# A two-block transformer on one core: attention's sums ahead of its turns, the mixers' low halves ahead of statistics and modulation, and the convolution as the last source of the mixers' output

## What is computed

```python
def gqa_mix(h_lat, h_ctx, ...):                 # block 1, layer 1: 8 heads of 128, 2 of k and v
    q_l = apply_rope(rms_norm(split_heads(qkv[..., :Q_DIM], N_HEADS), q_norm_g), cos, sin)
    k_all = jnp.concatenate([k_c, k_l], axis=2)
    y_lat = merge_heads(block_attend(q_l, k_all, v_all)) @ w_o

for l in range(DEPTH):                          # block 2
    mod = c_act @ ada_w[l] + ada_b[l]           # nine rows of 1024: shifts, scales, gates
    x = x + 0.5 * gt1 * _swiglu(_modulate(_rmsnorm(x, ffn1_norm[l]), sh1, sc1), ...)
    proj = _modulate(_rmsnorm(x, mix_norm[l]), sh2, sc2) @ mix_w_in[l]
    o_a = attention(rope(rmsnorm(a_q)), rope(rmsnorm(a_k)), a_v)   # 512 features, 8 heads of 64
    o_b = silu(group_layernorm(depthwise_conv31(a * sigmoid(g))))  # 256 features
    o_c = rmsnorm(gla(c_q, c_k, c_v, log_decay)) * silu(c_r)       # 256 features
    mixed = jnp.concatenate([o_a, o_b, o_c], axis=-1) @ mix_w_out[l]
    x = x + gt2 * mixed
    x = x + 0.5 * gt3 * _swiglu(_modulate(_rmsnorm(x, ffn2_norm[l]), sh3, sc3), ...)
```

## Time and profile before

| | us |
|---|---|
| median of 3 runs | 3186.99 |
| the runs | 3184.89 to 3188.21 |
| the profiled execution | 3188.7 |
| its span, first to last instruction | 3187.0 |
| PE busy in it | 3090.6 |

### The profile page before, as it was taken

One profiled execution on the slowest core, in us unless ns is written; L12 is line 12 of the kernel. 1 busy time (PEld: TensorE's weight loads), 2 busy tenths in 40 slices (PEclk: granted clock), 3 DMA queues, 4 the chain that ended last, 5 costly groups with the idle time before them and its releaser, 6 DMA issues.

```text
span 3187.0 us, 46876 instructions
## 1 busy us (share of the span) xinstructions
PE 3090.6 (97%) x19420; PEld 2751.5 (86%) x19420; DVE 2041.7 (64%) x2146; ACT 957.7 (30%) x1006; POOL 669.5 (21%) x616
## 2 busy tenths in 40 slices
PE   8999999999999999999997999999989999998999
PEld 5888889888888888888886798899879999997899
DVE  5844368666387434774556766675887758668664
ACT  2211122212222122221224433333533333354333
POOL 1311100224022010220102021330632313136110
PEclk9999999999999999999998999999999999999999
DMA  7633235332255332553523496685547868654464
GB/s 258 211 133 93 92 119 187 105 102 75 91 158 176 101 96 89 160 183 119 172 96 119 128 272 221 194 266 195 185 149 219 258 200 271 232 191 167 137 182 158
DMA packets 501669, 522.81 MB, mean 164 GB/s; under 512 B 15732, under 2 KB 433830, under 8 KB 501478
## 3 DMA queue, kind: packets, MB, share of 16 engines
q1 hardware_dynamic: 498536, 513.76, 50.4%
q0 software_dynamic: 2944, 6.32, 1.0%
HBM read 518.97 MB, written 1.05 MB: 163 GB/s over the span
## 4 chain that ended last, share of the span: by engine, by line
PE 86%; DVE 7%; POOL 3%; ACT 2%; DMA 1%; issue 1%; SPq 0%; DVEq 0%; ACTq 0%; POOLq 0%
PE ps L2191 29%; PE ps L2365 15%; PE ps L2277 15%; PE ps L2389 8%; PE ps L2219 6%; PE ps L2256 2%; DVE wl L1228 2%; PE ps L2235 1%; POOL wst L809 1%; PE ps L2662 1%; PE ps L2128 1%; POOL lnp L815 1%; PE ps L2303 1%; PE ps L2099 1%; DMA mraw<-in_ada_w 1%
## 5 line engine op out<-in xcount | busy, mean ns | idle before, releaser
L1228 DVE TENSOR_TENSOR wl<-wraw,wh 128x2048 fp32r<-128x2048 f32 x339 | 829.0, 2446 | 566.9 <-ACT wh L838 561.7
L838 ACT ACTIVATE wh<-wraw 128x2048 fp32r<-128x2048 f32 x341 | 652.5, 1913 | 945.7 <-PE ps L2277 387.5
L2191 PE MATMUL ps<-xh,wh 128*128 128x512 f32 (+1 forms) x1504 | 564.9, 376 | 0.5 <-DVE xl L1280 0.3
L2191 PE MATMUL ps<-xl,wh 128*128 128x512 f32 (+1 forms) x1504 | 552.7, 367 | 0.0
L2191 PE MATMUL ps<-xh,wl 128*128 128x512 f32 (+1 forms) x1504 | 551.3, 367 | 0.0
L2365 PE MATMUL ps<-xh,wh 128*128 128x258 f32 x1408 | 403.7, 287 | 5.3 <-DVE xl L1426 4.2
L2365 PE MATMUL ps<-xh,wl 128*128 128x258 f32 x1408 | 399.7, 284 | 0.0
L2365 PE MATMUL ps<-xl,wh 128*128 128x258 f32 x1408 | 399.3, 284 | 0.0
L673 POOL CAST hh<-ht 128x256 f32 (+1 forms) x176 | 140.1, 796 | 1227.1 <-DVE ht L1608 891.0
L1201 DVE SCALAR_TENSOR_TENSOR acc<-mraw,svec,acc 128x1024 f32<-128x1024 f32 x259 | 342.3, 1341 | 12.7 <-DMA mraw<-in_ada_w 5.2
L2191 PEld LDWEIGHTS ps<-xl,wh 128*128 128x128 f32 x1504 | 283.2, 188 | 49.3
(11 more groups left out here) (430 smaller groups left out, 5564.6 us busy)
## 6 DMA issues: line engine op xcount, KB each, us to landing
wraw<-in_ffn_w_in SPq DMA_DIRECT2D x352, 512.0 KB, 5.2
wraw<-in_ffn_w_out SPq DMA_DIRECT2D x176, 512.0 KB, 4.2
mraw<-in_ada_w SPq DMA_DIRECT2D x72, 1024.0 KB, 7.0
mraw<-in_w_mod SPq DMA_DIRECT2D x64, 1024.0 KB, 6.8
wraw<-in_gmlp_w_in SPq DMA_DIRECT2D x48, 512.0 KB, 4.5
wraw<-in_mix_w_in SPq DMA_DIRECT2D x48, 512.0 KB, 4.7
wraw<-in_gmlp_w_out SPq DMA_DIRECT2D x24, 512.0 KB, 3.9
first_w<-in_w_mod SPq DMA_DIRECT2D x8, 1024.0 KB, 11.6
```

The lines of the kernel that those rows point to most:

```text
L838: act.activation(wh[:, slot], wraw[:, slot], ACT.Copy).then_inc(whi_done, 1)
L1228: dve.tensor_tensor(wl[:, slot], wraw[:, slot], wh[:, slot].bitcast(F32), ALU.subtract)\
L2191: m = pe.matmul(ps[:, bank, 0:width], a, b, start=k == p == 0, stop=k == KD - 1 and p == 2)
```

## The change

- **Attention.** `queries(u)` falls into `query_sums(u)` and `query_turn(u)`; the sums stand one turn ahead, turns 1 and 2 stand together, turn 3 inside the head loop at head 0. POOL's two low halves (L796) go; DVE makes them inside the head loop at heads 2 and 4. ACT squares and splits earlier and runs a one-element exponential ahead of the first real one. The transposes of `q_1` write another bank.
- **Entry of block 2.** `keep_going` runs 20 products ahead of the wait for `y_evac` and 36 behind it, where 16 stood; `columns` stands behind the transposes.
- **Both mixers.** DVE's `split_next` of units 7, 9, 10, 11 and 12 stands ahead of sums, modulation or taps; DVE's taps (`taps(1)`) stand behind the split of unit 11; POOL's powers stand behind 7 and 10 taps (9 and 13 before). ACT takes over the copy and the squares of `o`, and the copies of `pt_c` and `pt_b`, and loads its tables ahead by one-element operations. `MIX_OUT` makes conv the last source; its statistics stand behind attention's low half. `columns(nxt, 1)` stands behind the scores, `columns(nxt, 2, 3)` behind `out(3)`. Modulation 10 stands between conv's low half and the last split, 12 and 13 behind that split. The next sublayer's order of input blocks (`MIXED`) changes.

```diff
-MIX_OUT = (3, 2, 0, 1)
+MIX_OUT = (3, 0, 1, 2)
-NATURAL, MIXED = tuple(range(8)), (0, 1, 4, 5, 6, 7, 2, 3)
+NATURAL, MIXED = tuple(range(8)), (0, 1, 2, 3, 6, 7, 4, 5)
-MIX_POOL_TAPS, MIX_DVE_TAPS = (9, 13, 24), (24, 28, 31)
+MIX_POOL_TAPS, MIX_DVE_TAPS = (7, 10, 24), (24, 28, 31)
...
-                    for i in (6, 7):
-                        u = s["n_unit"] + i
-                        pool.wait_ge(whi_done, u + 1)
-                        pool.tensor_tensor(wl[:, u % 2], wraw[:, u % 2], wh[:, u % 2].bitcast(F32), ALU.subtract)\
-                            .then_inc(wlo_done, 1)
...
+                    query_sums(0)
                     unit(3)
-                    queries(0)
+                    query_turn(0)
+                    query_sums(1)
                     unit(4)
-                    queries(1)
+                    query_sums(2)
+                    query_turn(1)
+                    query_turn(2)
                     maximum(0)
-                    queries(2)
+                    query_sums(3)
                     normalise(0)
                     maximum(1)
-                    queries(3)
                     normalise(1)
                     for h in range(HEADS):
                         if h + 2 < HEADS:
                             maximum(h + 2)
+                        if h == 0:
+                            query_turn(3)
+                        elif h == 2:
+                            unit(5)
+                        elif h == 4:
+                            unit(6)
                         if h in ATT_MODS:
                             mod_unit(nxt, 2, ATT_MODS.index(h))
...
-                    stage("o_copy", dve.tensor_copy(o_c, ps[:, 6].rearrange("p (t c) -> p t c", t=TT)))
-                    steps.link(dve.tensor_tensor(hx[:], o_c, o_c, ALU.mult))
...
                     stage("oc", dve.tensor_tensor(o_c, o_c, gg[:], ALU.mult))
-                    normalise("c", p_c, 0)
                     maximum("a", 0, 4, 12)
-                    MP.wait(dve, "conv", turn)
-                    steps.link(dve.tensor_copy(ctok.rearrange("p a b -> p (a b)"), ps[:, 7]))
-                    grp = ctok.rearrange("p t (g c) -> p (t g) c", c=64)
+                    low("gla", 6, (6,))
+                    normalise("b", p_b, 8)
+                    normalise("a", p_a[:], 12)
+                    split_next(u0 + 12)
+                    turned_weights("a", 0, slice(0, 2))
+                    low("att", 0, (0, 1))
                     for g in range(8):
                         m = steps.mark(dve.bn_stats(hst[:, g], grp[:, g]))
...
-                    split_next(u0 + 12)
+                    split_next(u0 + 13)
                     low("conv", 4, (2,))
+                    modulation(10)
+                    split_next(u0 + 14)
                     modulation(12)
-                    unit(13)
-                    low("att", 0, (0, 1))
-                    unit(14)
-                    unit(15)
+                    modulation(13)
...
+                    keep_going(3, 20)
                     pe.wait_ge(y_evac, s["n_group"])
+                    keep_going(3, 36)
+                    transposes(s)
                     columns(s, 2)
-                    keep_going(3, 16)
-                    transposes(s)
...
-                        MV.wait(pe, ("lo_gla", "lo_conv", "lo_att", "lo_att")[i], turn)
+                        MV.wait(pe, ("lo_gla", "lo_att", "lo_att", "lo_conv")[i], turn)
...
-                        if i == 2:
-                            columns(nxt, 2, 3)
...
-                    for i in range(1, 4):
-                        out(i)
+                    out(1)
+                    out(2)
+                    MA.wait(pe, "conv", turn)
+                    MP.done("convt", outputs_turned(512, 2))
+                    out(3)
+                    columns(nxt, 2, 3)
```

More of the change, by code:

```diff
@@ L1026, in _ @@
                     unit(3, False)
+                    square(1)
                     split_next(u0 + 4)
-                    square(1)
-                    copy_heads(0)
                     unit(4, False)
                     square(2)
+                    copy_heads(0)
+                    split_next(u0 + 5)
+                    act.activation(nrm1[:, 31:32], ones[:, 0:1], ACT.Exp)
+                    unit(5, False)
+                    square(3)
                     copy_heads(1)
                     exps(0)
-                    unit(5)
-                    square(3)
                     copy_heads(2)
@@ L1150, in _ @@
                     unit(10)
+                    MP.wait(act, "o", turn)
+                    stage("o_copy", act.activation(om[:, :, 768:1024], ps[:, 6].rearrange("p (t c) -> p t c", t=TT), ACT.Copy))
+                    stage("o_sq", act.activation(hx[:], om[:, :, 768:1024], ACT.Square))
                     exps("c", 2, p_c, 0)
-                    unit(11)
+                    split_next(u0 + 11)
                     exps("b", 4, p_b, 8)
+                    act.activation(table_scrap[:, 0:1], ones[:, 0:1], ACT.Silu)
+                    unit(11, False)
+                    act.activation(table_scrap[:, 1:2], ones[:, 0:1], ACT.Exp)
                     MP.wait(act, "omt", turn)
@@ L1156, in _ @@
                     exps("a", 0, p_a[:], 12)
+                    act.activation(table_scrap[:, 2:3], ones[:, 0:1], ACT.Silu)
+                    MP.wait(act, "pt_c", turn)
+                    MA.done("pt_c", act.activation(pt0[:, :, :, 0:P], ps[:, 2:4].rearrange("p r (h q) -> p r h q", h=4), ACT.Copy))
                     unit(12)
+                    MP.wait(act, "pt_b", turn)
+                    act.activation(pt0[:, :, 2:4, P:2 * P], ps[:, 2].rearrange("p (r h q) -> p r h q", r=2, h=2), ACT.Copy)
+                    MA.done("pt_b", act.activation(pt1[:, :, 2:4], ps[:, 3].rearrange("p (r h q) -> p r h q", r=2, h=2), ACT.Copy))
+                    MP.wait(act, "pv", turn)
+                    high("att", 0, (0, 1))
+                    unit(13)
                     MV.wait(act, "o_conv", turn)
@@ L1161, in _ @@
                     high("conv", 4, (2,))
-                    unit(13)
-                    MP.wait(act, "pv", turn)
-                    high("att", 0, (0, 1))
                     unit(14)
@@ L1976, in _ @@
                     turn_heads(0)
+                    split_next(u0 + 6)
+                    sum_squares(1)
                     modulation(5)
-                    sum_squares(1)
-                    unit(6)
-                    taps(1)
                     turn_heads(1)
                     split_next(u0 + 7)
-                    split_next(u0 + 8)
-                    modulation(7)
                     MA.wait(dve, "decays", turn)
@@ L2006, in _ @@
                     stage("kt_t", op)
-                    unit(9)
+                    modulation(8)
+                    split_next(u0 + 9)
+                    mod_end(nxt, 1, 6, 488)
                     MP.wait(dve, "scores", turn)
@@ L2026, in _ @@
                     stage("states", op)
-                    unit(10)
+                    split_next(u0 + 10)
+                    taps(1)
+                    modulation(9)
                     maximum("c", 2, 8, 0)
-                    MP.wait(dve, "o", turn)
+                    MA.wait(dve, "o_sq", turn)
                     o_c = om[:, :, 768:1024]
-                    stage("o_copy", dve.tensor_copy(o_c, ps[:, 6].rearrange("p (t c) -> p t c", t=TT)))
-                    steps.link(dve.tensor_tensor(hx[:], o_c, o_c, ALU.mult))
                     groups = nrm_g.rearrange("p (t h) -> p t h", t=TT)
@@ L2059, in _ @@
                     stage("stats", dve.tensor_tensor(grp, grp, hmv[:, :, 0:1].broadcast_to([P, 8, 64]), ALU.subtract))
-                    low("gla", 6, (6,))
-                    MP.wait(dve, "pt_c", turn)
-                    MV.done("pt_c", dve.tensor_copy(pt0[:, :, :, 0:P], ps[:, 2:4].rearrange("p r (h q) -> p r h q", h=4)))
-                    normalise("b", p_b, 8)
                     dve.wait_ge(rstd_ready, n_power[0])
@@ L2801, in _ @@
                     MP.done("pt_a", turn_weights(p_a[:], 0))
-                    MV.wait(pe, "pt_b", turn)
-                    MA.wait(pe, "conv", turn)
-                    MP.done("convt", outputs_turned(512, 2))
+                    MA.wait(pe, "pt_b", turn)
                     MV.wait(pe, "pt_a", turn)
```

79 lines of the change are left out of this document (42 added, 37 removed).

## The result

| | before | changed |
|---|---|---|
| median, us | 3185.94 (4 runs) | 3164.93 (4 runs) |
| the runs | 3183.42 to 3188.21 | 3163.78 to 3168.58 |
| span of the profiled execution | 3187.0 | 3166.8 |

The ratio is 0.9936 with a 95% interval from 0.9919 to 0.9953: 21 us, or 0.6%, faster, where 19 were forecast. The profiled executions differ by 20.2 us.

What follows compares the result with a forecast made beforehand. PE was taken to bound the kernel, busy 3090.6 of 3187.0 us. Attention -8.2, entry of block 2 +1.2, mixers -8.5 and -6.0, late loads +2.5 summed to -19.0, giving 3168 us, range 3155 to 3182.

Steps and rivals of the forecast that it cites:

- the new wait: Attention, head 5: DVE waits for the `mraw` load queued behind the weight unit awaiting head 4's low half; 5.0 us.
- The other waits: Attention: PE waits expected to remain, 0.8 + 1.5 at transposes, 2.8 for `ptb`, 3.0 at heads with modulation steps.
- the excess of 8.5 us: Attention: DVE turn operations lengthened by 4.3 + 4.2 us beside POOL's low halves, ahead of the division PE awaits.
- helps little: Entry of block 2: products buy clock for columns and transposes, of little help since the next products wait for DVE.
- The wait of 4.3 us: Front of both mixers: PE's wait for a low half behind sums and modulation goes with the split ahead; 4.3 us.
- the list: Waits per mixer: first out 0.7, turned weights 1.5, attention's halves 2.9, out(3) 6.2, gla transposes 1.3, turned keys 0.6, ffn 1.0.
- the late loads: Next ffn behind each mixer: weights requested some 2 us later; 1.25 us per mixer, +2.5 in all, bounds 0 and 4.
- the prediction's recipe: Attention and both mixers: low clock's cost taken as busy time times the missing share; 7.9, 10.9 and 7.6 us.
- GpSimd's taps: Rival: POOL's taps become the mixers' bound, margin about 2 us, each mixer loses 4, total 3176; chance 0.15.
- Long operations with another cause: Rival: attention's long operations are not POOL's doing; 7.3 us wait stays, attention about +2, total 3178; chance 0.07.
- One chain at the end: Rival: mixer tail's conv source, modulation 10, last split in series; slower if 12.7 us more per mixer, 3195; chance 0.05.
- The case worked out for that rival: Mixer tails: `mraw` and two units land in series, three landings of 6.8 us, 8 already summed; 2 x 13.5 more, 3195.

## Why the prediction was right, and where it was not

**The whole.** 3164.9 against 3168, well inside 3155 to 3182, mostly by the forecast's own mechanisms; -20.2 between the executions against -19.0. That the sum came within 1.2 us is in part luck: two errors of 3 us with opposite signs stand in it (the ffn at the entry, the second mixer), two of 2 more outside the changed places (up to attention, the two ffn), and the first mixer of the one execution compared was at the slow end of its 169.8 to 174.4.

**Attention, -8.2 against -7.3 (attention alone: -8.1).** Idle time fell by 7.1 us where 6.2 were forecast, low clock by 0.8 where 2.0 were: the new wait had slow work of its own behind it. That wait, worked out from the issue and landing rows, was put at 5.0; VectorE waited 5.24 and TensorE 4.5. The other waits were 0.3 and 1.5 where 0.8 and 1.5 were expected, 2.5 for 2.8, and 2.4 between later heads for 3.0. What the working missed is that the two halves of one step cancel: the excess of 8.5 us read from the earlier trace rows is real, but the move that removed it also made the wait at head 5. The kernel with the halves on GpSimd took 99.2, no more than the changed one. Both terms were in the sum, which is why it held; that they nearly cancel, and that the load could be taken out of the way (8.3 us less in the execution measured), was not seen.

**Entry of block 2, +1.2 against +1.2.** 56 pairs at 0.112 us, taken from the earlier trace rows, gave the transposes at 12.5 us behind the last product; they stood at 2015.95, 12.5 behind 2003.44. The step that failed is that nothing was booked behind the entry: the clock there "helps little", says the prediction. The ffn behind it was 3.3 us shorter, a term that was put at 0. In the means of the kernels it goes with the order of the columns, by some 2.5 us, and not with the products; that is a correlation over thirteen executions and not a shown cause. The 1.2 is itself made of two parts that I did not see apart: the order gives 0.3 to 1.9 us back, and the 40 products cost 3.1. I looked for the clock's price only in the entry itself, and the ffn behind it is where the executions differ.

**Mixers, front.** The wait of 4.3 us went in both, as forecast.

**Mixers, tail.** Of the list, 0.7 was 0.77, 1.5 was 1.47, 2.9 was 2.46, 6.2 was 6.19 and 1.3 was 1.31. The 0.6 for the turned keys did not come, but 0.74 to 0.76 ahead of the scores did. Missed was 0.74 for a split ahead of the third product, and the next ffn's first wait was 2.4 and 2.0, not 1.0; here the load behind modulation 10 was named but its price too low by half. I had booked the late loads again at 1.25 us per mixer inside the ffn; those two terms together (1.0 + 1.25) are the 2.0 to 2.4 that were measured, and the two ffn between the mixers did not get longer. Behind the second mixer 1.2 us came, as much as was booked, but the kernel with the mixers' part alone took 199.4 there, so the late loads are not shown to be its cause. The wait at the ffn (1.4 and 1.0 more than forecast) and the split (0.74) are the terms of the tail that were too small.

**Mixers, waits against clock: the terms that were mis-sized.** First mixer -9.7 against -8.5, second -3.2 against -6.0. By the table of slow work, idle time fell by 2.5 and 1.2 us where 4.6 and 2.8 were forecast. Low clock fell by 7.2 and 1.5 us where 3.9 and 3.2 were. So the waits gave less than expected in both, for the reasons above, and the clock decided: its cost after was 3.6 and 5.7, where 7.0 and 4.4 were forecast by subtracting from what each mixer had before. The first mixer's number came near by two errors of 2 and 3 us with opposite signs; in the second both pointed one way. Much of the clock's gain in the first belongs to the execution of before: the same mixer took 169.8 us in another kernel, with 12.1 us of slow work instead of 21.5, and from there the change would have gained 5. Mean clock times busy time, the prediction's recipe, put the kernel before at 10.9 and 7.6 us, near the 10.7 and 7.2 counted; after the change it gives 147.94 x 0.04 = 5.9 and 149.44 x 0.04 = 6.0 against the 3.6 and 5.7 counted, since much of the low clock there fell on idle time, and the mean clock is rounded.

**Rivals.** GpSimd's taps: not the bound, but 1.0 us away in the first mixer and 2.5 in the second, where I said 2; the run with 5 us more of GpSimd shows 4.6 and 4.7 us per mixer, near the price of 4 that I gave for 6 us. Long operations with another cause: excluded by the rows of the run with the halves put back. One chain at the end: it existed with its 6.2 us in each mixer, and moving four transposes removed it; it stayed far below the 12.7 us more that would have turned the sign. The case worked out for that rival does not reach its own threshold either: three landings of 6.8 us less the 8 in the sum are 12 us per mixer, not the 13.5 used, and give 3192.

## What to carry to other kernels

When work is moved off an engine that holds a buffer's release, follow the release as well as the work: here the low half made later held up, through SyncE's queue, a load that another engine needed (4.5 us of TensorE's time and 2.4 of low clock behind it). When a wait is a chain of several steps, first ask where the chain starts; the transposes that started it had their input 7.5 us earlier, and moving those four instructions was worth 12 us, more than half of the whole change. Count low clock as the work that ran in it, not as mean clock times busy time once much of it falls on idle time, and look at more than one execution before a change is credited with it: in a mixer whose code did not change slow work lay between 12.1 and 21.5 us.

## What the runs showed of the hardware that I had not expected

- A VectorE operation with one tensor input in SBUF is held up by GpSimd too: the two divisions `sg<-sg,den` took 5.13 us beside GpSimd's 4.65, against 0.88 alone. The Trainium skill ("SBUF — State Buffer", Who interferes with whom) says that such a form can enter a mode with two ports and then contend, when its operands meet the conditions of that mode. This row agrees, for float32 with one scalar per partition: taken one by one in the trace the two took 0.50 and 4.71, and only the first had begun before GpSimd's operation.
- GpSimd's multiplication of 128 x 256 took 1.0 us each when five stood in a row (4.98), while in the tap chain of the kernel before the same form took up to 3.90 us (at 2272.94); how much of the difference is VectorE's was not tried.
- The first ffn of block 2, whose code is the same in all kernels, took from 207.8 to 213.4 us with the same instructions; TensorE did 3.3 us of slow work (granted clock 0.50) in the shortest and 13.5 in the longest, which by the estimate above is 5.1 of the 5.6 us between them.
